# FFN gate/up products: one 512-wide matmul for [high | low] of x, one 256-wide for the low weights

## The chip, the cores and the metric

One core of one Trainium2 chip. The metric is the device time of one execution in microseconds (us), the median of several runs. The inputs and outputs are fp32 arrays in HBM, and the whole program is one launch.

## What is computed

The reference is two stacked blocks on 256 tokens of width 1024. The first is a mixer (neighbourhood attention, Fourier and convolution heads) and a mixture of 32 experts; the second has two layers, each with a feed-forward part (FFN), attention, and another FFN. The change touches the four FFNs only:

```python
def swiglu(x, w_in, w_out):
    gate, up = jnp.split(x @ w_in, 2, axis=-1)      # w_in: 1024 x 5632
    return (jax.nn.silu(gate) * up) @ w_out         # w_out: 2816 x 1024

for i in range(2):
    x = x + 0.5 * swiglu(rmsnorm(x, norm_gains[i, 0]), ffn_w_in[i, 0], ffn_w_out[i, 0])
    ...                                             # dilated, then latent attention
    x = x + 0.5 * swiglu(rmsnorm(x, norm_gains[i, 2]), ffn_w_in[i, 1], ffn_w_out[i, 1])
```

## The kernel before

Large products are done in three passes of a shorter format (fp32r): each fp32 operand is split into a high part, rounded to fp32r, and a low part, the rest; the product is high times high plus high times low plus low times high. For x the parts are XH and XL (128 partitions x 8 k-tiles x 256 tokens each); for the weights they are HI and LO, made from RAW, the buffer that the DMA fills. RAW, HI and LO have two slots, j = 0 and 1.

`ffn` works on chunks of 128 hidden channels. There are 22 of them in an FFN: FF_TWICE = 11 steps i of a loop, two slots j each, so 88 chunks in the four FFNs. A chunk has 128 gate columns and 128 up columns of w_in (2048 elements per partition of the slot, q = 0 for gate and 1 for up) and 128 rows of w_out (1024 elements per partition).

- SyncE (`sync`, L144) issues the loads: as soon as `gu_low` of slot j is done, the next gate/up weights of that slot (L153), and after the low part of the down weights, the next down weights (L156).
- ScalarE (ACT) makes the high parts: `gu_high` (L162, 2048 wide) and the down part (L175, 1024 wide), which waits until the matmuls of the down product of the same slot, one step earlier, no longer need HI. `silu(j, i)` then takes silu of the gate half out of PSUM (L180, into SG), waits for the product with up, and makes its high part HH (L182).
- VectorE (DVE) makes the low parts: `gu_low` (L166) and the down part (L199). `hidden(j, i)` multiplies SG by the up half in PSUM (L205, into H) and makes the low part HL (L207).
- TensorE (PE) runs `gate_up(j, i)`: for q = 0 and 1 and each of the 8 k-tiles three matmuls 256 tokens wide (L232), 48 in all, into one PSUM bank, 4 or 5, gate in one half and up in the other. `down(j, i)` is 12 matmuls 512 wide (L242), which accumulate in banks 0 to 3 over all chunks.

The order on each engine is written out by hand. In a step of the loop:

- PE: gate_up(0, i), down(1, i - 1), gate_up(1, i), down(0, i)
- ACT: gu_high(0, i), down part of high(0, i), silu(1, i - 1), gu_high(1, i), down part of high(1, i), silu(0, i)
- DVE: the low parts and `hidden` in the same order as ACT.

So ACT, after the down product of one slot, makes that slot's down high part, then handles the hidden values of the other slot, and only then makes the gate/up high part for the chunk after next on PE. At the end of an FFN, ACT and DVE handle chunk (1, 10) while PE runs down(0, 10), and down(1, 10) comes last; then DVE adds 0.5 times the result to X (L221). Ahead of each FFN and attention, `norm_and_transpose` squares X on ACT (L94), scales it, transposes it on PE (L123, through banks 6, 7, 2 and 3) and writes XH (ACT, L97) and XL (DVE, L113).

The semaphores named in the change: gu_used (gate_up done), silu (ACT to DVE), h_done (DVE to ACT, and to PE as "the bank is free"), hh_done, hl_done (DVE to PE: HH and HL are ready), dn_used (down done).

Of the kernel before, what the change touches and what calls it, by code (L numbers as in the profile page):

```python
# [16 lines left out]
ALU = mybir.AluOpType  # L17
ACT = mybir.ActivationFunctionType
AX = mybir.AxisListType
f32 = mybir.dt.float32  # L20
f32r = mybir.dt.float32r
i32 = mybir.dt.int32

D = 1024
KT = D // 128
T = 256
# [35 lines left out]
def at_least(eng, sem, value):  # L62

    if not isinstance(value, int) or value > 0:
        eng.wait_ge(sem, value)
# [63 lines left out]
def ffn(nc, M, n_norm, f, w_in, w_out, raw_free):  # L129


    XH, XL, X, PS, s = M.XH, M.XL, M.X, M.PS, M.ffn
    Y = PS[:, 0:4, :]
    GU = [PS[:, 4, :], PS[:, 5, :]]
    w_in_v = w_in.rearrange("(k p) n -> p k n", p=128)
    w_out_v = w_out.rearrange("(c p) n -> c p n", p=128)
    u0 = FF_TWICE * f
    a, v, e, sp = nc.scalar, nc.vector, nc.tensor, nc.sync

    def gu(buf, j):  # L140
        return buf[:, j, 0:2048].rearrange("p (q k n) -> p q k n", q=2, k=KT)

    def dn(buf, j):
        return buf[:, j, 2048:3072]  # L144

    def sync():
        for j in range(2):
            raw_free(sp, j)
        with sp.Fori(0, FF_TWICE) as i:
            for j in range(2):  # L150
                sp.wait_ge(s.gu_lo[j], i + (u0 + 1))
                for q in range(2):
                    sp.dma_start(gu(M.RAW, j)[:, q], w_in_v[:, :, bass.ds(i * 256 + (j * 128 + q * FF), 128)]  # L153
                                 ).then_inc(s.gu_in[j], 16)
                sp.wait_ge(s.dn_lo[j], i + (u0 + 1))
                sp.dma_start(dn(M.RAW, j), w_out_v[bass.ds(i * 2 + j, 1)].rearrange("a p n -> p (a n)")  # L156
                             ).then_inc(s.dn_in[j], 16)

    def gu_high(j, i):
        a.wait_ge(s.gu_in[j], i * 32 + (32 * u0 + 32))  # L160
        a.wait_ge(s.gu_used[j], i + (u0 + 1))
        a.activation(M.HI[:, j, 0:2048], M.RAW[:, j, 0:2048], ACT.Copy).then_inc(s.gu_hi[j], 1)  # L162

    def gu_low(j, i):
        v.wait_ge(s.gu_hi[j], i + (u0 + 1))
        v.tensor_tensor(M.LO[:, j, 0:2048], M.RAW[:, j, 0:2048], M.HI[:, j, 0:2048].bitcast(f32),  # L166
                        ALU.subtract).then_inc(s.gu_lo[j], 1)

    def act():
        def high_parts(j, i, first=False):  # L170
            if not first:
                gu_high(j, i)
            a.wait_ge(s.dn_in[j], i * 16 + (16 * u0 + 16))
            a.wait_ge(s.dn_used[j], i + (u0 + 1))
            a.activation(dn(M.HI, j), dn(M.RAW, j), ACT.Copy).then_inc(s.dn_hi[j], 1)  # L175

        def silu(j, i):
            a.wait_ge(s.gu_used[j], i + (u0 + 2))
            a.wait_ge(s.h_done[j], i + (u0 + 1))
            a.activation(M.SG[:, j], GU[j][:, 0:T], ACT.Silu).then_inc(s.silu[j], 1)  # L180
            a.wait_ge(s.h_done[j], i + (u0 + 2))
            a.activation(M.HH[:, j], M.H[:, j], ACT.Copy).then_inc(s.hh_done[j], 1)  # L182

        high_parts(0, 0, first=True)
        high_parts(1, 0)
        silu(0, 0)
        with a.Fori(1, FF_TWICE) as i:
            high_parts(0, i)
            silu(1, i - 1)
            high_parts(1, i)  # L190
            silu(0, i)
        silu(1, FF_TWICE - 1)

    def dve():
        def low_parts(j, i, first=False):
            if not first:
                gu_low(j, i)
            v.wait_ge(s.dn_hi[j], i + (u0 + 1))
            v.tensor_tensor(dn(M.LO, j), dn(M.RAW, j), dn(M.HI, j).bitcast(f32),  # L199
                            ALU.subtract).then_inc(s.dn_lo[j], 1)  # L200

        def hidden(j, i):
            v.wait_ge(s.silu[j], i + (u0 + 1))
            v.wait_ge(s.dn_used[j], i + (u0 + 1))
            v.tensor_tensor(M.H[:, j], M.SG[:, j], GU[j][:, T:2 * T], ALU.mult).then_inc(s.h_done[j], 1)  # L205
            v.wait_ge(s.hh_done[j], i + (u0 + 1))
            v.tensor_tensor(M.HL[:, j], M.H[:, j], M.HH[:, j].bitcast(f32), ALU.subtract).then_inc(s.hl_done[j], 1)  # L207

        low_parts(0, 0, first=True)
        low_parts(1, 0)  # L210
        hidden(0, 0)
        with v.Fori(1, FF_TWICE) as i:
            low_parts(0, i)
            hidden(1, i - 1)
            low_parts(1, i)
            hidden(0, i)
        hidden(1, FF_TWICE - 1)
        for n in range(4):
            v.wait_ge(s.y_done, 4 * f + n + 1)
            xs = X[:, n // 2, 512 * (n % 2):512 * (n % 2) + 512]  # L220
            v.scalar_tensor_tensor(xs, Y[:, n], 0.5, xs, ALU.mult, ALU.add).then_inc(M.x_ready, 1)  # L221

    def pe():
        def gate_up(j, i, first=False):
            e.wait_ge(s.gu_lo[j], i + (u0 + 2))
            e.wait_ge(s.h_done[j], i + (u0 + 1))
            for q in range(2):
                for k in range(KT):
                    if first and q == 0:
                        e.wait_ge(M.xl_done, KT * n_norm + k + 1)  # L230
                    for n, (w, x) in enumerate([(M.HI, XH), (M.HI, XL), (M.LO, XH)]):
                        m = e.matmul(GU[j][:, T * q:T * q + T], gu(w, j)[:, q, k, :], x[:, k, :],  # L232
                                     start=(k == 0 and n == 0), stop=(k == KT - 1 and n == 2))
            m.then_inc(s.gu_used[j], 1)

        def down(j, i, first=False, last=False):
            e.wait_ge(s.dn_lo[j], i + (u0 + 2))
            e.wait_ge(s.hl_done[j], i + (u0 + 1))
            for t in range(NT):
                for q in range(2):  # L240
                    for n, (h, w) in enumerate([(M.HH, M.HI), (M.HH, M.LO), (M.HL, M.HI)]):
                        m = e.matmul(Y[:, 2 * t + q], h[:, j, 128 * t:128 * t + 128],  # L242
                                     dn(w, j)[:, 512 * q:512 * q + 512],
                                     start=first and n == 0, stop=last and n == 2)
                        if last and (t, q, n) == (1, 1, 1):
                            m.then_inc(s.dn_used[j], 1)
                    if last:
                        m.then_inc(s.y_done, 1)
            if not last:
                m.then_inc(s.dn_used[j], 1)  # L250

        gate_up(0, 0, first=True)
        gate_up(1, 0)
        down(0, 0, first=True)
        with e.Fori(1, FF_TWICE) as i:
            gate_up(0, i)
            down(1, i - 1)
            gate_up(1, i)
            down(0, i)
        down(1, FF_TWICE - 1, last=True)  # L260

    return sync, act, dve, pe, lambda: gu_high(0, 0), lambda: gu_low(0, 0)
# [1802 lines left out]
def program(nc, A, out):  # L2065

    with ExitStack() as c:
        M = Names()

        def sb(name, shape, dtype=f32):  # L2070
            return c.enter_context(nc.sbuf_tensor(name, shape, dtype))
# [12 lines left out]
        M.X = sb("X", [128, NT, D])  # L2084
        M.ID = sb("ID", [128, 128])
        M.GC = sb("GC", [128, N_GC])
        M.XH, M.XL = sb("XH", [128, KT, T], f32r), sb("XL", [128, KT, T], f32r)
        M.RAW = sb("RAW", [128, 2, SLOT])
        M.HI, M.LO = sb("HI", [128, 2, SLOT], f32r), sb("LO", [128, 2, SLOT], f32r)
        M.R = sb("R", [128, 11776])  # L2090
# [17 lines left out]
        def carve(*shape, at=None):  # L2108
            n = math.prod(shape)
            start = end[0] if at is None else at  # L2110
            end[0] = start + n
            assert end[0] <= ARENA
            ap = arena[:, start:start + n]
            if len(shape) == 2:
                return ap.rearrange("p (a b) -> p a b", a=shape[0])
            if len(shape) == 3:
                return ap.rearrange("p (a b c) -> p a b c", a=shape[0], b=shape[1])
            if len(shape) == 4:
                return ap.rearrange("p (a b c d) -> p a b c d", a=shape[0], b=shape[1], c=shape[2])
            return ap  # L2120
# [41 lines left out]
        xn = carve(NT, D, at=0)  # L2162
        ot = carve(KT, T, at=0)
        base = end[0]
        junk, M.SG, M.H = carve(D), carve(2, T), carve(2, T)
        beyond = lambda at, n: M.R[:, KT * D + at:KT * D + at + n]
        M.a_SC = [[carve(384, at=base), carve(768)], [beyond(0, 384), beyond(384, 768)]]
        M.a_PT = [[carve(384), carve(384)], [beyond(1152, 384), beyond(1536, 384)]]
# [234 lines left out]
```

## Time and profile before

| | us |
|---|---|
| median of 3 runs | 2085.25 (2079.49 to 2085.77) |
| the profiled execution | 2084.06 |
| its span, first to last instruction | 2082.2 |

The profiled execution has 1.86 us outside its span. The four FFNs lie at about 768 to 958, 1289 to 1479, 1487 to 1676 and 1888 to 2078 us of the span. In the rows below, "busy" of PE counts pipelined matmuls whose recorded durations overlap, so the pace of PE is read from start to start or from the pieces of the chain, not from the mean duration. PEld is the weight load that goes ahead of each matmul. What stands in brackets at the end of a timeline row is the idle time before the instruction and who ended it.

### The profile page before, as it was taken

How to read it: one execution, taken by the hardware profiler on the slowest of the kernel's cores; microseconds unless marked ns; L12 is line 12 of the kernel's file. 1: busy time of each engine (PE TensorE's matmuls, PEld its weight loads, DVE VectorE, ACT ScalarE, POOL GpSimd, SP SyncE). 2: the span in 40 equal slices, each digit the busy share in tenths (PEclk: the TensorE clock that was granted, in tenths of full speed). 3: DMA queues.
4: the chain of work that ended last, by engine and by line, in shares of the span. 5: the costliest groups of instructions: out<-in, count | busy, mean ns of one | idle time of the engine just before them, and what ended most of it. 6: DMA issues, size and time to landing. Idle time of an engine off the chain costs nothing.

```text
span 2082.2 us, 30499 instructions
## 1 busy us (share of the span) xinstructions
PE 1906.7 (92%) x11508; PEld 1439.0 (69%) x11508; DVE 887.5 (43%) x1391; ACT 734.5 (35%) x1190; POOL 94.9 (5%) x88
## 2 busy tenths in 40 slices
PE   6999699999998959997999998999899977788999
PEld 2875434434333339997999985999899965547998
DVE  4242301111111054545777764454544435525554
ACT  3352212111111134444555543444444434424443
POOL 1000000000000000000111110000000001100000
PEclk8999799999999989999999999999999988879999
DMA  9851699999999956664745442666566550105663
GB/s 366 302 210 63 227 393 393 396 392 395 396 391 396 394 165 183 181 196 121 233 122 152 121 121 60 183 181 181 151 182 183 176 193 0 33 28 152 181 181 111
DMA packets 377285, 441.85 MB, mean 212 GB/s; under 512 B 14469, under 2 KB 273029, under 8 KB 373893
## 3 DMA queue, kind: packets, MB, share of 16 engines
q1 hardware_dynamic: 374776, 431.60, 62.2%
q0 software_dynamic: 2176, 8.39, 1.2%
q10 hardware_dynamic: 272, 1.05, 0.1%
q8 instruction: 38, 0.62, 0.1%
q14 instruction: 23, 0.19, 0.0%
HBM read 439.94 MB, written 1.05 MB: 212 GB/s over the span
## 4 chain that ended last, share of the span: by engine, by line
PE 78%; DMA 10%; ACT 4%; DVE 3%; SPq 2%; issue 2%; POOL 1%; ACTq 0%; POOLq 0%; DVEq 0%
PE PS L232 24%; PE PS L242 11%; PE PS L429 10%; DMA R<-w_up 8%; PE PS L1857 4%; PE PS L1533 4%; PE PS L1835 3%; PE PS L1806 3%; PE PS L1825 3%; SPq L1692 2%; PE PS L757 1%; PE PS L709 1%; PE PS L1642 1%; PE PS L835 1%; ACT ARENA L1723 1%
## 5 line engine op out<-in xcount | busy, mean ns | idle before, releaser
L232 PE MATMUL PS<-XH,HI 128*128 128x256 f32 x1408 | 399.8, 284 | 0.6 <-DVE LO L166 0.6
L232 PE MATMUL PS<-XL,HI 128*128 128x256 f32 x1408 | 398.6, 283 | 0.0
L232 PE MATMUL PS<-XH,LO 128*128 128x256 f32 x1408 | 398.5, 283 | 0.0
L232 PEld LDWEIGHTS PS<-XH,HI 128*128 128x128 f32 x1408 | 270.3, 192 | 4.7 <-DVE LO L166 1.0
L232 PEld LDWEIGHTS PS<-XL,HI 128*128 128x128 f32 x1408 | 270.2, 192 | 3.8
L232 PEld LDWEIGHTS PS<-XH,LO 128*128 128x128 f32 x1408 | 270.2, 192 | 0.0
L166 DVE TENSOR_TENSOR LO<-RAW,HI 128x2048 fp32r<-128x2048 f32 x88 | 201.7, 2292 | 118.8 <-ACT HI L162 118.8
L1777 DVE TENSOR_TENSOR ARENA<-PS,ARENA 128x512 f32<-128x512 f32 x64 | 44.2, 691 | 375.6 <-PE PS L1835 375.6
L175 ACT ACTIVATE HI<-RAW 128x1024 fp32r<-128x1024 f32 x88 | 93.4, 1062 | 295.0 <-PE PS L242 295.0
L199 DVE TENSOR_TENSOR LO<-RAW,HI 128x1024 fp32r<-128x1024 f32 x88 | 107.8, 1225 | 196.8 <-ACT HI L175 196.5
L162 ACT ACTIVATE HI<-RAW 128x2048 fp32r<-128x2048 f32 x88 | 167.8, 1907 | 6.3 <-DMA RAW<-ffn_w_in 6.3
L1825 PE MATMUL PS<-R,ARENA 128*64 128x512 f32 x640 | 144.8, 595 | 13.3 <-DMA R<-w_up 13.3
L242 PE MATMUL PS<-LO,HH 128*128 128x512 f32 x352 | 139.0, 395 | 0.0
L242 PE MATMUL PS<-HI,HL 128*128 128x512 f32 x352 | 139.0, 395 | 0.0
L242 PE MATMUL PS<-HI,HH 128*128 128x512 f32 x352 | 139.0, 395 | 0.0
L429 PE MATMUL PS<-HI,XL 128*128 128x384 f32 x384 | 134.8, 351 | 2.2 <-DVE LO L416 2.2
L429 PE MATMUL PS<-HI,XH 128*128 128x384 f32 x384 | 129.6, 338 | 0.0
L429 PE MATMUL PS<-LO,XH 128*128 128x384 f32 x384 | 129.4, 337 | 0.0
L1825 PEld LDWEIGHTS PS<-R,ARENA 128*64 128x64 f32 x640 | 44.6, 137 | 110.5 <-issue 77.0
L1825 PE MATMUL PS<-RAW,ARENA 128*64 128x512 f32 x384 | 86.7, 594 | 4.0 <-DMA RAW<-w_up 2.4
L1728 ACT ACTIVATE ARENA<-PS 128x512 f32<-128x512 f32 x16 | 9.6, 597 | 225.2 <-PE PS L1825 225.2
L416 DVE TENSOR_TENSOR LO<-RAW,HI 128x3072 fp32r<-128x3072 f32 x24 | 80.5, 3354 | 12.6 <-ACT HI L411 12.6
(310 smaller groups left out, 2946.0 us busy)
## 6 DMA issues: line engine op xcount, KB each, us to landing
RAW<-ffn_w_in SPq DMA_DIRECT2D x176, 512.0 KB, 5.1
RAW<-ffn_w_out SPq DMA_DIRECT2D x88, 512.0 KB, 3.5
R<-w_gate SPq DMA_DIRECT2D x80, 512.0 KB, 11.4
R<-w_up SPq DMA_DIRECT2D x80, 512.0 KB, 10.5
R<-w_down SPq DMA_DIRECT2D x80, 512.0 KB, 12.4
RAW<-a_w_in SPq DMA_DIRECT2D x72, 512.0 KB, 5.3
R<-w_ada SPq DMA_DIRECT2D x24, 1024.0 KB, 7.6
RAW<-w_gate SPq DMA_DIRECT2D x48, 512.0 KB, 13.0
```

The costliest lines, as they stand in the source:

```text
L162: a.activation(M.HI[:, j, 0:2048], M.RAW[:, j, 0:2048], ACT.Copy).then_inc(s.gu_hi[j], 1)
L166: v.tensor_tensor(M.LO[:, j, 0:2048], M.RAW[:, j, 0:2048], M.HI[:, j, 0:2048].bitcast(f32), ALU.subtract).then_inc(s.gu_lo[j], 1)
L175: a.activation(dn(M.HI, j), dn(M.RAW, j), ACT.Copy).then_inc(s.dn_hi[j], 1)
L199: v.tensor_tensor(dn(M.LO, j), dn(M.RAW, j), dn(M.HI, j).bitcast(f32), ALU.subtract).then_inc(s.dn_lo[j], 1)
L232: m = e.matmul(GU[j][:, T * q:T * q + T], gu(w, j)[:, q, k, :], x[:, k, :], start=(k == 0 and n == 0), stop=(k == KT - 1 and n == 2))
L242: m = e.matmul(Y[:, 2 * t + q], h[:, j, 128 * t:128 * t + 128], dn(w, j)[:, 512 * q:512 * q + 512], start=first and n == 0, stop=last and ...
L416: v.tensor_tensor(M.LO[:, slot], M.RAW[:, slot], M.HI[:, slot].bitcast(f32), ALU.subtract).then_inc(s.w_lo[slot], 1)
L429: m = e.matmul(FB[t][:, 0:AW], x[:, k, 128 * t:128 * t + 128], part(w, slot)[:, k].rearrange("p g n -> p (g n)"), start=(k == 0 and n == 0 ...
L1533: mm = e.matmul(FB[n % 2][:, 256 * m:256 * m + 256], l, r, start=(k == 0 and q == 0), stop=(k == KT - 1 and q == 2))
L1806: m = e.matmul(PS[:, 4 + k // 4, 128 * (k % 4):128 * (k % 4) + 128], XN[:, t, 128 * k:128 * k + 128], M.OH[:, t], start=t == 0, stop=t == 1)
L1825: mm = e.matmul((GB, UB)[m // 4][CAP * x:CAP * x + CAP], M.XG[:, k, CAP * x:CAP * x + CAP], w[:, x, kk, :], start=k == 0, stop=k == KT - 1)
L1857: mm = e.matmul(PS[CAP * x:CAP * x + CAP, 2 + q, :], M.HT[:, 128 * f + CAP * x:128 * f + CAP * x + CAP], w[:, x, 512 * q:512 * q + 512], s ...
```

## The change

The 256-wide pair "high weights times high x" and "high weights times low x" becomes one matmul 512 wide, whose moving operand is [XH | XL] of a k-tile, now adjacent in one buffer XHL. Its left half of the bank collects high times high, its right half high times low. The third product, low weights times high x, stays 256 wide and accumulates into the left half. Gate and up so need a bank each, and the two slots take banks 4 and 5, 6 and 7. The halves still have to be added: ACT first copies the two right halves (gate and up, 512 elements per partition) out of PSUM into GH, DVE adds the two left halves from PSUM to them in place, ACT takes silu of the gate part, now in SBUF and in place, and DVE multiplies it by the up part, also in SBUF. HH and HL follow as before. The counts of silu and h_done go up by 2 per chunk instead of 1.

```diff
-    GU = [PS[:, 4, :], PS[:, 5, :]]
+    GU = [PS[:, 4 + 2 * j:6 + 2 * j, :] for j in range(2)]
...
         def silu(j, i):
             a.wait_ge(s.gu_used[j], i + (u0 + 2))
-            a.wait_ge(s.h_done[j], i + (u0 + 1))
-            a.activation(M.SG[:, j], GU[j][:, 0:T], ACT.Silu).then_inc(s.silu[j], 1)
-            a.wait_ge(s.h_done[j], i + (u0 + 2))
+            at_least(a, s.hl_done[j], i + u0)
+            a.activation(M.GH[:, j], GU[j][:, :, T:2 * T], ACT.Copy).then_inc(s.silu[j], 1)
+            a.wait_ge(s.h_done[j], i * 2 + (2 * u0 + 2))
+            a.activation(M.SG[:, j], M.SG[:, j], ACT.Silu).then_inc(s.silu[j], 1)
+            a.wait_ge(s.h_done[j], i * 2 + (2 * u0 + 3))
             a.activation(M.HH[:, j], M.H[:, j], ACT.Copy).then_inc(s.hh_done[j], 1)
...
         def hidden(j, i):
-            v.wait_ge(s.silu[j], i + (u0 + 1))
+            v.wait_ge(s.silu[j], i * 2 + (2 * u0 + 1))
+            v.tensor_tensor(M.GH[:, j], GU[j][:, :, 0:T], M.GH[:, j], ALU.add).then_inc(s.h_done[j], 1)
+            v.wait_ge(s.silu[j], i * 2 + (2 * u0 + 2))
             v.wait_ge(s.dn_used[j], i + (u0 + 1))
-            v.tensor_tensor(M.H[:, j], M.SG[:, j], GU[j][:, T:2 * T], ALU.mult).then_inc(s.h_done[j], 1)
+            v.tensor_tensor(M.H[:, j], M.SG[:, j], M.H[:, j], ALU.mult).then_inc(s.h_done[j], 1)
...
         def gate_up(j, i, first=False):
             e.wait_ge(s.gu_lo[j], i + (u0 + 2))
-            e.wait_ge(s.h_done[j], i + (u0 + 1))
+            at_least(e, s.h_done[j], i * 2 + 2 * u0)
...
-                    for n, (w, x) in enumerate([(M.HI, XH), (M.HI, XL), (M.LO, XH)]):
-                        m = e.matmul(GU[j][:, T * q:T * q + T], gu(w, j)[:, q, k, :], x[:, k, :],
-                                     start=(k == 0 and n == 0), stop=(k == KT - 1 and n == 2))
+                    both = lambda: e.matmul(GU[j][:, q], gu(M.HI, j)[:, q, k, :], M.XHL[:, k].rearrange("p a t -> p (a t)"),
+                                            start=k == 0, stop=k == KT - 1)
+                    rest = lambda: e.matmul(GU[j][:, q, 0:T], gu(M.LO, j)[:, q, k, :], XH[:, k, :], start=False, stop=False)
+                    for product in ((both, rest) if k < KT - 1 else (rest, both)):
+                        m = product()
...
-        M.XH, M.XL = sb("XH", [128, KT, T], f32r), sb("XL", [128, KT, T], f32r)
+        M.XHL = sb("XHL", [128, KT, 2, T], f32r)
+        M.XH, M.XL = M.XHL[:, :, 0], M.XHL[:, :, 1]
...
-        junk, M.SG, M.H = carve(D), carve(2, T), carve(2, T)
+        junk, M.GH = carve(D), carve(2, 2, T)
+        M.SG, M.H = M.GH[:, :, 0], M.GH[:, :, 1]
```

## Rows read from the trace of the kernel before

**Rows 1.** The page: busy times of the engines.

```profile
PE 1906.7 (92%) x11508; PEld 1439.0 (69%) x11508; DVE 887.5 (43%) x1391; ACT 734.5 (35%) x1190; POOL 94.9 (5%) x88
```

**Rows 2.** Stretches: us, then busy (instructions) by engine, PE clock, DMA.

```profile
790.00:940.00 150.00, 150.00 (x1053) 140.31 (x1052) 74.95 (x71) 62.51 (x70) 0.00 (x0) 1.00 0.62 184
```

**Rows 3.** The chain that ended last, in order of time: start, length, what.

```profile
792.01 5.75 PE PS L232 x48
797.76 2.80 PE PS L242 x12
```

**Rows 4.** Timeline of PE, 384-wide fp32r matmuls, the first and last of 21.

```profile
1059.67 0.34 PE L429 MATMUL PS<-HI,XH 128*128 128x384 f32 x1
...
1063.14 0.33 PE L429 MATMUL PS<-LO,XH 128*128 128x384 f32 x1
```

**Rows 5.** Timeline of PE and PEld where two gate_up products begin.

```profile
902.73 0.19 PEld L232 LDWEIGHTS PS<-XH,HI 128*128 128x128 f32 x1
902.96 0.28 PE L232 MATMUL PS<-XH,HI 128*128 128x256 f32 x1
...
911.27 0.19 PEld L232 LDWEIGHTS PS<-XH,HI 128*128 128x128 f32 x1
911.50 0.28 PE L232 MATMUL PS<-XH,HI 128*128 128x256 f32 x1
```

**Rows 6.** Timeline of ACT between those two.

```profile
903.22 1.06 ACT L175 ACTIVATE HI<-RAW 128x1024 fp32r<-128x1024 f32 x1 [3.56 <-PE PS L242]
904.19 0.36 ACT L180 ACTIVATE ARENA<-PS 128x256 f32<-128x256 f32 x1
905.90 0.42 ACT L182 ACTIVATE HH<-ARENA 128x256 fp32r<-128x256 f32 x1 [1.35 <-DVE ARENA L205]
906.23 1.90 ACT L162 ACTIVATE HI<-RAW 128x2048 fp32r<-128x2048 f32 x1
```

**Rows 7.** Timeline of DVE, from the same down part on, and the next chunk's L166.

```profile
904.31 1.22 DVE L199 TENSOR_TENSOR LO<-RAW,HI 128x1024 fp32r<-128x1024 f32 x1 [2.33 <-ACT HI L175]
905.46 0.41 DVE L205 TENSOR_TENSOR ARENA<-ARENA,PS 128x256 f32<-128x256 f32 x1
906.35 0.43 DVE L207 TENSOR_TENSOR HL<-ARENA,HH 128x256 fp32r<-128x256 f32 x1 [0.48 <-ACT HH L182]
908.16 2.29 DVE L166 TENSOR_TENSOR LO<-RAW,HI 128x2048 fp32r<-128x2048 f32 x1 [1.38 <-ACT HI L162]
...
916.79 2.29 DVE L166 TENSOR_TENSOR LO<-RAW,HI 128x2048 fp32r<-128x2048 f32 x1 [1.46 <-ACT HI L162]
```

**Rows 8.** Timeline at the start of the first FFN, where PE does wait for L166.

```profile
772.32 2.29 DVE L166 TENSOR_TENSOR LO<-RAW,HI 128x2048 fp32r<-128x2048 f32 x1 [0.57 <-ACT HI L162]
...
774.66 0.38 PE L232 MATMUL PS<-XH,HI 128*128 128x256 f32 x1 [0.25 <-DVE LO L166]
774.88 0.28 PE L232 MATMUL PS<-XL,HI 128*128 128x256 f32 x1
```

**Rows 9.** Groups by form: the shapes of the added operations on ACT and DVE.

```profile
L1728 ACT ACTIVATE ARENA<-PS 128x512 f32<-128x512 f32 x16 | 9.6, 597 | 225.2 <-PE PS L1825 225.2
L862 ACT ACTIVATE ARENA<-ARENA 128x256 f32<-128x256 f32 x8 | 3.3, 410 | 0.1
L1777 DVE TENSOR_TENSOR ARENA<-PS,ARENA 128x512 f32<-128x512 f32 x64 | 44.2, 691 | 375.6 <-PE PS L1835 375.6
```

**Rows 10.** Timeline of ACT and DVE at the end of the second FFN.

```profile
1472.38 0.38 ACT L180 ACTIVATE ARENA<-PS 128x256 f32<-128x256 f32 x1 [2.59 <-PE PS L232]
...
1473.70 0.43 DVE L207 TENSOR_TENSOR HL<-ARENA,HH 128x256 fp32r<-128x256 f32 x1 [0.48 <-ACT HH L182]
1475.88 2.79 DVE L221 SCALAR_TENSOR_TENSOR X<-PS,X 128x512 f32<-128x512 f32 x4 [1.75 <-PE PS L242]
```

**Rows 11.** Timeline of ACT after the first FFN.

```profile
958.00 2.76 ACT L411 ACTIVATE HI<-RAW 128x3072 fp32r<-128x3072 f32 x1 [5.07 <-DMA RAW<-a_w_in]
```

**Rows 12.** The page's DMA issues: count, KB each, median us to landing.

```profile
RAW<-ffn_w_in SPq DMA_DIRECT2D x176, 512.0 KB, 5.1
```

## The prediction

> **What bounds the kernel now.** I read the page first: PE is busy 92% of the span, DVE 43%, ACT 35% [rows 1]. That only says where to look. The stretch inside the first FFN shows PE busy without a gap at the full clock of 2.4 GHz, DVE half and ACT 42% of the time [rows 2]. The chain of waits there holds nothing but PE: 48 matmuls of gate_up in 5.75 us, 12 of down in 2.80 us, again and again [rows 3]. So 256-wide matmuls go at 5.75 / 48 = 119.8 ns and 512-wide ones at 2.80 / 12 = 233.3 ns from start to start, and a chunk takes 8.55 us. The mean durations in the groups are longer because the matmuls overlap; no saving can be read from them. With PE never waiting, the next question is how near the nearest wait is. That is in the timelines of ACT and DVE between two gate_up starts [rows 5 to 7], and it decides this case.
>
> **What PE gains.** Per k-tile and per gate or up, two 256-wide matmuls (239.6 ns) become one 512-wide (233.3 ns, the pace of L242, which is the same format with the same weight load ahead of each matmul). That is 6.3 ns; times 16 it is 0.10 us per chunk, times 88 chunks 8.9 us. A chunk would take 8.44 us on PE. The gain is small because it is only the fixed part of a matmul: columns stream at 2.4 GHz in 106.7 ns per 256, so the fixed part is 13.1 ns at 256 columns, 173.5 - 160 = 13.5 ns at 384 (3.47 us for 20 intervals [rows 4]), but 20 ns at 512. If the new 512-wide matmul had the fixed part of the 384-wide one it would take 226.8 ns and the gain would be 12.8 ns, 18 us in all. I take 233.3, since it is a row of the very width; the other end goes into a rival.
>
> The Trainium skill (TensorE: Matmul & The Clock Gate, section Back-to-back issue gap) has two figures for this. One is a fixed part of 2.5 ns at any width, by which a pair would save 2.5 ns, 3.5 us in all; the trace has 13 to 20 ns. The other is a sustained 131 ns for a 512-wide matmul among weight loads; the trace has 233.3 ns and so disagrees. By that figure PE would save 108.6 ns a pair, 153 us in all, before ACT and DVE hold it up.
>
> **What ACT and DVE get more of.** Per chunk ACT has a copy of 512 elements from PSUM instead of a silu of 256 from PSUM, and a silu of 256 in SBUF besides: 0.60 and 0.41 us [rows 9] instead of 0.36 [rows 6]. DVE has one add of 512 with a PSUM operand more, 0.69 us, and its multiply reads SBUF only, like L207, 0.43 instead of 0.41 us [rows 9, 7]. In sums that is 57 us on ACT and 62 us on DVE, and by engine load it would be hidden: DVE would be busy some 5.0 of 8.5 us. But it lies in series ahead of the weights' split, so what counts is the path.
>
> **The path.** Take the gate_up that starts at 902.96 [rows 5], call this moment D: the down product before it has ended and freed its high weights. ACT starts the down high part at 903.22 and then silu of the other slot [rows 6]; DVE makes the down low part, ending 905.53, and multiplies, ending 905.87 [rows 7]; ACT makes HH from 905.90 and starts gu_high at 906.23; DVE starts gu_low at 908.16 and ends at 910.45 [rows 6, 7]. These weights are for the gate_up at 911.50, whose first weight load is issued at 911.27 [rows 5]. Handing over from one engine to the other takes 0.03 us; two operations without a wait on one engine overlap by 0.03 to 0.09 us.
>
> After the change: the copy runs 904.19 to 904.79, still under the down low part (hidden; if the low part were shorter by 0.75 us it would show). Then add 905.46 to 906.15, silu 906.18 to 906.59, multiply 906.62 to 907.04, HH from 907.07, gu_high from 907.40, gu_low 909.33 to 911.62. That is 1.17 us later: 0.69 (add) + 0.03 + 0.41 (silu) + 0.03 + 0.01 (multiply). PE, 0.10 us quicker, would want the weights at 911.17; today they are there 0.8 us before the load, then 0.45 us after it. What does PE lose? Where PE waits for L166 today, the low part ends at 774.61, the first matmul starts at 774.66 and the second at 774.88 instead of 0.12 us later [rows 8]: a late start costs 0.05 + 0.10 us behind the end of L166. So the next gate_up counts as started at 911.62 + 0.15 = 911.77, or L = 8.81 us after D, against 8.44 that PE would need by itself. In the other slot D is 911.50 and L166 starts at 916.79 [rows 5, 7]; L166 ends 7.58 us after D instead of 7.49, since the loop's branch is passed on ACT there, so L = 8.90 us.
>
> **How a late path adds up.** The path starts at the end of one down product and ends at the gate_up after the next one. If s is the time between two ends of down products, the next s is 8.44 + max(0, L - s). One late gate_up lengthens s and so gives the next path more room. The first late one in an FFN is gate_up(1, 1), by 0.37 us; after that each pair of chunks loses about 0.37 us together while both are late and 0.46 us once the lateness has settled on one slot. Iterated over the 19 gate_ups that can be late in an FFN, this gives 4.0 us, 16 us in four FFNs. So the loop goes at about 8.44 + 0.20 = 8.64 us per chunk, not 8.55. The first two gate_ups of an FFN are not reached by the path: their ACT and DVE work runs under 5.65 us of gate_up(1, 0) and 2.80 us of down(0, 0).
>
> **The end of an FFN.** The last chunk's hidden values are made under down(0, 10) alone. Today silu starts 1472.38 and HL ends 1474.13 [rows 10]; down(0, 10) starts about 0.2 us before that silu, while the last gate_up matmul drains, and down(1, 10) 2.80 us later, at about 1474.97 with its weight load at 1474.74, so 0.6 us of slack. After: copy 0.60, add 0.69, silu 0.41, multiply 0.43, HH 0.42, HL 0.43 and five handovers of 0.03 to 0.04 make 3.15 us, HL ends at 1475.53, PE is late by 0.05 + 0.10 and effectively starts at 1475.68, 0.7 us late. It passes on to the X updates (L221) and the next stage in three FFNs; after the first one ACT waits for a DMA until 958.00, and X is done at 957.93 and has until 960.7 [rows 11], so there it costs nothing. 3 x 0.7 = 2 us. The hidden values inside the loop are no such place: HL ends at 906.78 now, 907.95 then, and down wants them at 902.73 + 5.65 = 908.38, 0.4 us later.
>
> **What else moves.** The wait of PE for a free PSUM bank is on the add of one chunk of the same slot earlier, long done. Behind ACT's new wait for the add stand silu, HH and gu_high; behind DVE's new wait for silu stand the multiply, HL and gu_low: that is the path above. SyncE's loads follow gu_low and land 5.1 us after their issue [rows 12]; gu_high of the same slot is two chunks on, 17.1 us after gu_high and so 12.9 us after the end of gu_low today, and both of its ends move together, so 1.2 us later costs nothing. XHL changes addresses, not counts, for the attention products. Banks 6 and 7 are read by XH and XL before gate_up(0, 0) can end. Each of these I take as 0, and none has a row that would make it a gain.
>
> **The sum.** 2084.06 - 8.9 + 16 + 2 = 2093.2 us for an execution like the profiled one, which lies 1.2 us under the median of the runs shown; 2094 for the median. Its bounds from rows: a silu of 0.36 (PSUM row) instead of 0.41 and an overlap of 0.03 more give 0.08 x 40 = 3 us less; 0.1 us more of handover per chunk gives 4 us more. Its own range is 2090 to 2099.
>
> **Rivals.**
> - *The 512-wide matmul has the 13.5 ns of the 384-wide row.* For it: two widths agree. Against: the row of the same width. PE gains 18 us and wants 8.34 us a chunk, but the path does not move, so each of the 40 pairs waits 0.10 us more, 20 us instead of 16: 2084 - 18 + 20 + 2 = 2088, or 2089 for the median. No measurable change.
> - *The path is not late.* This decides if the delay of gu_low stays under 0.80 us (8.44 against the 7.49 + 0.15 of today), for which the add and the silu would have to take 0.73 us together instead of 1.10. Then 2084.06 - 8.9 + 2 or less = 2077. Faster. No row is that short, so it gets little.
> - *No gain on PE.* In the new stream a 512-wide and a 256-wide matmul alternate, which the trace does not show. If the weight load behind the 256-wide one is not hidden, or the 512-wide one takes 240 ns, the gain is 0; a chunk wants 8.55 us, stalls are L - 8.55 = 0.26 to 0.35 a pair, 12 us, and the sum is 2084 + 12 + 2 = 2098. Slower.
> - *The path is longer than the sum of its rows.* An in-place operation or the two-bank PSUM operand costs more than a plain one: 0.25 us more on the path adds 0.25 x 40 = 10 us, 2103. Slower.
> - *The new 512-wide matmul goes at the pace of a 256-wide one.* At 119.8 ns PE would want 8.55 - 16 x 0.12 = 6.63 us a chunk, and the path of about 8.85 us would set (8.85 + 6.63) / 2 = 7.74 us, 0.81 us less in each of some 80 chunks, 65 us faster, 2020. Twelve 512-wide matmuls in 2.80 us speak against it. The skill's sustained 131 ns (same page and section) is a figure of this kind; the trace disagrees with it.
>
> **Chances.** Forecast 0.50, 384-like pace 0.17, path not late 0.10, no gain on PE 0.10, longer path 0.12, far faster 0.01. A measurement of this kernel tells about 0.3%, 6.3 us, from no change: slower means over 2091.5. Of the forecast nine tenths lie above that. Slower 0.45 + 0.10 + 0.11 = 0.64 or so, same 0.26, faster 0.10. The range runs from 2081, which takes in the 384-like pace with a shorter path, to 2102.
>
> **What would show it.** In the profile after: L232 in two forms, the 512-wide at 233 ns start to start and the 256-wide at 120; the chain in the FFNs no longer PE alone but passing through L166, gu_high, HH, the multiply, silu and the add; PE waiting for L166 some 55 times by 0.2 to 0.4 us; the add at 0.69, the copy at 0.60, the silu at 0.41 us; the weight load of down(1, 10) waiting for HL. I am wrong if PE's pieces are still gapless, or if the two forms together take less than 345 or more than 360 ns.

## The result and the profile after

| | before | after |
|---|---|---|
| median, us | 2081.4 (2079.49 to 2085.77, 5 runs) | 2094.4 (2093.54 to 2099.85, 5 runs) |
| the profiled execution, its span | 2084.06, 2082.2 | 2099.85, 2098.0 |

The changed kernel is slower: its time is 1.0063 of that of before, interval 1.0044 to 1.0083. With the runs that the experiments below added, the median of before settled at 2084.2 to 2084.6, so by medians the loss is some 10 to 13 us, 0.5 to 0.6%. The forecast was 2094, 0.4 to 0.5% slower. The profiled execution of the changed kernel is the slowest of its five.

The page of the changed kernel, busy times and the groups that answer to [rows 1] and to L232 (columns: busy us, mean ns of one; idle us before and who ended it):

```profile
PE 1911.9 (91%) x10100; PEld 1364.3 (65%) x10100; DVE 949.1 (45%) x1479; ACT 790.9 (38%) x1278; POOL 95.0 (5%) x88
L235 PE MATMUL PS<-XHL,HI 128*128 128x512 f32 x1408 | 503.6, 402 | 11.0 <-DVE LO L166 10.6
L237 PE MATMUL PS<-XHL,LO 128*128 128x256 f32 x1408 | 367.1, 281 | 0.0
```

L235 is the new 512-wide matmul, L237 the 256-wide one. PE now has idle time that L166, the low parts of the gate/up weights, ends; before it was busy without a gap in an FFN [rows 2]. DVE got 62 us of work more and ACT 56, as the rows had it, and both are still under half busy.

The view of the line L235 has the idle time before its matmuls and before its weight loads in one count, so many late starts stand in it twice:

```profile
its engine sat idle before it (us, times) until:
  DVE LO L166: 27.0, 63
  issue: 16.6, 27
```

By the timelines, start to start, 50 of the 80 gate_ups that follow a down product begin late.

The chain that ended last, one gate_up start to the next (start, length, what; answers to [rows 3]). It used to hold PE alone:

```profile
900.13 1.07 ACT HI L175
...
902.37 0.69 DVE ARENA L206
903.06 0.02 issue
903.08 0.43 ACT ARENA L182
903.51 0.02 issue
903.53 0.44 DVE ARENA L209
...
904.38 1.93 ACT HI L162
906.31 0.02 issue
906.34 2.30 DVE LO L166
908.64 0.12 issue
908.76 0.49 PE PS L235
...
914.64 2.81 PE PS L248 x12
```

Once the late starts have settled on one slot, the chain leaves PE every second chunk at the end of a down product and goes down part (L175), add (L206), silu (L182), multiply (L209), high part (L162), low part (L166) before it is back on PE. These are the forecast's links in the forecast's order. The timelines of ACT and DVE in the next chunk answer to [rows 6] and [rows 7]:

```profile
908.54 1.06 ACT L175 ACTIVATE HI<-RAW 128x1024 fp32r<-128x1024 f32 x1 [2.24 <-PE PS L248]
909.51 0.58 ACT L180 ACTIVATE ARENA<-PS 128x512 f32<-128x512 f32 x1
911.50 0.42 ACT L182 ACTIVATE ARENA<-ARENA 128x256 f32<-128x256 f32 x1 [1.41 <-DVE ARENA L206]
...
910.78 0.68 DVE L206 TENSOR_TENSOR ARENA<-PS,ARENA 128x512 f32<-128x512 f32 x1
911.95 0.43 DVE L209 TENSOR_TENSOR ARENA<-ARENA 128x256 f32<-128x256 f32 x1 [0.48 <-ACT ARENA L182]
...
914.67 2.29 DVE L166 TENSOR_TENSOR LO<-RAW,HI 128x2048 fp32r<-128x2048 f32 x1 [1.38 <-ACT HI L162]
```

The copy ends at 910.09, under the down low part, as was said; the add took 0.68 us, the silu 0.42, the multiply 0.43, the handovers 0.02 to 0.04.

And PE where it waits (answers to [rows 5] and [rows 8]):

```profile
908.06 0.39 PE L248 MATMUL PS<-HI,HL 128*128 128x512 f32 x1
...
908.76 0.49 PE L235 MATMUL PS<-XHL,HI 128*128 128x512 f32 x1 [0.32 <-DVE LO L166]
...
909.09 0.28 PE L237 MATMUL PS<-XHL,LO 128*128 128x256 f32 x1
```

Without the wait the gate_up would have started at 908.06 + 0.23 = 908.29. It started 0.47 us later, and its second matmul came 0.33 us behind the first instead of 0.23: 0.57 us lost. (The 0.32 us in brackets is less than 0.47, because it counts from the end of a matmul's recorded duration of 0.39 us, and matmuls in a stream follow each other after 0.23.)

**Where the difference of the two profiled executions lies.** From the start of the first to the start of the last matmul of an FFN, by the timelines:

| FFN | before, us | after, us | change |
|---|---|---|---|
| 1 | 188.44 | 191.63 | +3.2 |
| 2 | 188.73 | 191.65 | +2.9 |
| 3 | 188.84 | 193.49 | +4.7 |
| 4 | 188.50 | 192.23 | +3.7 |

That is 14.5 us. The stages behind the first and the third FFN are 1.8 and 0.7 us shorter than before, and 3.8 us more lie ahead of the first FFN (it starts at 772.2 instead of 768.4). None of these three can be put down to the change: over the ten kernels profiled here the first FFN starts between 767.6 and 773.9 us, with no regard to what was changed in them. The stage behind it, which waits for a DMA [rows 11], took 332.0 us before, but 329.3 in before_reordered and 330.2 in layout_only, whose FFNs are as fast; that DMA took 8.49 us in the profile before, 6.61 in before_reordered and 7.25 in the changed kernel. So the time of the four FFNs, 14.5 us more, is a cleaner measure of the loss than a difference of medians.

### The profile page after: what moved, and what is told of

Its sections match the earlier page's. It is cut to its first block, busy times and chain, and to the rows that moved or that the text cites. A ratio compares the mean times of both kernels' runs of the same rounds, so it can differ in the third digit from the quotient of the medians.

```text
span 2098.0 us, 28187 instructions
## 1 busy us (share of the span) xinstructions
PE 1911.9 (91%) x10100; PEld 1364.3 (65%) x10100; DVE 949.1 (45%) x1479; ACT 790.9 (38%) x1278; POOL 95.0 (5%) x88
## 4 chain that ended last, share of the span: by engine, by line
PE 64%; ACT 9%; DMA 9%; DVE 9%; issue 4%; SPq 2%; POOL 1%; ACTq 0%; DVEq 0%; POOLq 0%
PE PS L235 10%; PE PS L435 9%; DMA R<-w_up 8%; PE PS L248 6%; PE PS L237 5%; PE PS L1863 4%; PE PS L1539 4%; DVE LO L166 4%; ACT HI L162 3%; PE PS L1841 3%; PE PS L1812 3%; PE PS L1831 3%; SPq L1698 2%; ACT HI L175 2%; PE PS L763 1%
## 5 line engine op out<-in xcount | busy, mean ns | idle before, releaser
L235 PE MATMUL PS<-XHL,HI 128*128 128x512 f32 x1408 | 503.6, 402 | 11.0 <-DVE LO L166 10.6
L237 PE MATMUL PS<-XHL,LO 128*128 128x256 f32 x1408 | 367.1, 281 | 0.0
L235 PEld LDWEIGHTS PS<-XHL,HI 128*128 128x128 f32 x1408 | 259.8, 189 | 82.6 <-issue 16.6
L237 PEld LDWEIGHTS PS<-XHL,LO 128*128 128x128 f32 x1408 | 267.0, 190 | 12.7
L166 DVE TENSOR_TENSOR LO<-RAW,HI 128x2048 fp32r<-128x2048 f32 x88 | 201.7, 2292 | 119.8 <-ACT HI L162 119.8
L435 PE MATMUL PS<-HI,XHL 128*128 128x384 f32 x768 | 212.3, 344 | 2.2 <-DVE LO L422 2.2
L175 ACT ACTIVATE HI<-RAW 128x1024 fp32r<-128x1024 f32 x88 | 93.3, 1060 | 205.9 <-PE PS L248 205.9
L162 ACT ACTIVATE HI<-RAW 128x2048 fp32r<-128x2048 f32 x88 | 167.9, 1908 | 5.4 <-DMA RAW<-ffn_w_in 4.8
L1831 PE MATMUL PS<-R,ARENA 128*64 128x512 f32 x640 | 144.8, 595 | 13.2 <-DMA R<-w_up 13.2
L435 PEld LDWEIGHTS PS<-HI,XHL 128*128 128x128 f32 x768 | 141.0, 189 | 8.0 <-issue 4.6
L435 PE MATMUL PS<-LO,XHL 128*128 128x384 f32 x384 | 129.3, 337 | 0.0
L1863 PE MATMUL PS<-R,ARENA 128*64 128x512 f32 x320 | 71.8, 595 | 10.4 <-ACT ARENA L1738 10.4
L182 ACT ACTIVATE ARENA<-ARENA 128x256 f32<-128x256 f32 x88 | 36.8, 418 | 117.6 <-DVE ARENA L206 117.6
```

The lines of the kernel that those rows point to most:

```text
L235: both = lambda: e.matmul(GU[j][:, q], gu(M.HI, j)[:, q, k, :], M.XHL[:, k].rearrange("p a t -> p (a t)"), start=k == 0, stop=k == KT - 1)
L237: rest = lambda: e.matmul(GU[j][:, q, 0:T], gu(M.LO, j)[:, q, k, :], XH[:, k, :], start=False, stop=False)
L435: m = e.matmul(FB[t][:, 0:AW], x[:, k, 128 * t:128 * t + 128], part(w, slot)[:, k].rearrange("p g n -> p (g n)"), start=(k == 0 and n == 0 ...
L1831: mm = e.matmul((GB, UB)[m // 4][CAP * x:CAP * x + CAP], M.XG[:, k, CAP * x:CAP * x + CAP], w[:, x, kk, :], start=k == 0, stop=k == KT - 1)
L1863: mm = e.matmul(PS[CAP * x:CAP * x + CAP, 2 + q, :], M.HT[:, 128 * f + CAP * x:128 * f + CAP * x + CAP], w[:, x, 512 * q:512 * q + 512], s ...
```

## The experiments

The theory is the one of the forecast: PE gains about 0.12 us a chunk, and the longer path from ACT and DVE takes more than that back. The rivals: the new stream of matmuls is no quicker in itself; any operation added to ACT or DVE costs its own time; the new layout of XH and XL costs something elsewhere. "A pair" below is the time from one gate_up to the next of the same slot, two chunks, read from the timelines in the first FFN, where it has settled. "FFNs" is the sum of the four spans from first to last matmul start, as in the table above.

| kernel | median, us | ratio to before (interval) | pair, us | FFNs, us | PE |
|---|---|---|---|---|---|
| before | 2084.2 to 2084.6 | | 17.09 | 754.5 | old stream |
| changed | 2094.4 | 1.0063 (1.0044 to 1.0083) | 17.40 | 769.0 | new |
| pe_only | 2075.29 | 0.9952 (0.9938 to 0.9965) | 16.84 | 743.7 | new |
| path_only | 2102.76 | 1.0086 (1.0072 to 1.0099) | 17.53 | 775.1 | old |
| after_reordered | 2076.66 | 0.9960 (0.9946 to 0.9973) | 16.84 | 746.8 | new |
| before_reordered | 2084.28 | 0.9999 (0.9990 to 1.0008) | 17.09 | 754.1 | old |
| dose1 | 2085.24 | 1.0005 (0.9995 to 1.0015) | 17.09 | 754.3 | old |
| dose3 | 2109.26 | 1.0119 (1.0102 to 1.0136) | 17.74 | 780.3 | old |
| waits_swapped | 2094.51 | 1.0058 (1.0043 to 1.0073) | 17.25 to 17.35, not settled | 768.5 | new |
| layout_only | 2084.86 | 1.0004 (0.9995 to 1.0013) | 17.09 | 754.2 | old |

### PE's part alone

```diff
...
-            a.activation(M.GH[:, j], GU[j][:, :, T:2 * T], ACT.Copy).then_inc(s.silu[j], 1)
-            a.wait_ge(s.h_done[j], i * 2 + (2 * u0 + 2))
-            a.activation(M.SG[:, j], M.SG[:, j], ACT.Silu).then_inc(s.silu[j], 1)
...
+            a.activation(M.SG[:, j], GU[j][:, 0, 0:T], ACT.Silu).then_inc(s.silu[j], 1)
...
-            v.tensor_tensor(M.GH[:, j], GU[j][:, :, 0:T], M.GH[:, j], ALU.add).then_inc(s.h_done[j], 1)
...
-            v.tensor_tensor(M.H[:, j], M.SG[:, j], M.H[:, j], ALU.mult).then_inc(s.h_done[j], 1)
+            v.tensor_tensor(M.H[:, j], M.SG[:, j], GU[j][:, 1, 0:T], ALU.mult).then_inc(s.h_done[j], 1)
...
```

The waits, left out here, count as before the change. The right halves are computed and never read.

> The changed matmuls (512-wide and 256-wide, two banks a slot) with the ACT and DVE work of the kernel before: silu reads the left half of the gate bank, the multiply the left half of the up bank. Left out: the right halves, high weights times low x, are computed by PE but never read. Theory (the path through ACT and DVE costs more than PE gains): with the old path PE never waits, a chunk takes 8.43 us (5.63 for gate_up, 2.80 for down), 88 chunks x 0.12 = 9 to 10 us faster than before, about 0.4 to 0.5%. Rival (the alternating 512- and 256-wide stream is no quicker in itself): 0 to 3 us from before. Rival (512-wide at a much better pace): over 20 us faster.

8.9 us faster by the medians, ratio 0.9952; 10.8 us by the FFNs. Two down products in the chain of waits (start, length, what):

```profile
845.02 2.79 PE PS L244 x12
...
853.44 2.79 PE PS L244 x12
```

They stand 8.42 us apart, against 8.55 before [rows 3]: 5.63 us for gate_up, which is 351.9 ns for a 512-wide and a 256-wide matmul where three 256-wide ones took 359.4. The new stream is quicker in itself, by 7.5 ns where the pace of L242 gave 6.3; the first rival is out.

### The path alone

```diff
-                    both = lambda: e.matmul(GU[j][:, q], ...
-                    rest = lambda: e.matmul(GU[j][:, q, 0:T], ...
...
+                    for n, (w, x, h) in enumerate([(M.HI, XH, 0), (M.HI, XL, T), (M.LO, XH, 0)]):
+                        m = e.matmul(GU[j][:, q, h:h + T], gu(w, j)[:, q, k, :], x[:, k, :],
+                                     start=(k == 0 and n == 0), stop=(k == KT - 1 and n == 2))
```

> The changed ACT and DVE work (copy of the right halves, add, silu in SBUF, multiply), layout and banks, but all three products as 256-wide matmuls as before, high times low x into the right half of the bank. Theory: PE wants 8.55 us a chunk again, the path does not move, so the stalls shrink a little but the gain is gone; a pair of chunks takes about 17.09 + 0.45 us where it has settled, 15 to 20 us slower than before, 5 to 8 us slower than the changed kernel. Rival (the time is lost in the new matmul stream, not in the path): the path alone costs 0 to 3 us.

18.5 us slower than before, 8 us slower than the changed kernel. The chain of waits:

```profile
871.25 1.93 ACT HI L162
873.17 0.02 issue
873.20 2.31 DVE LO L166
875.50 0.12 issue
875.63 6.02 PE PS L236 x48
881.65 2.81 PE PS L246 x12
```

It is the chain of the changed kernel with the old 48 matmuls in it. So the loss is in the path, whatever PE does, and PE's gain is real but half used: the pair is 17.53 us here and 17.40 in the changed kernel, 0.13 us less, where the same matmuls without waits save 0.25.

### The same work in another order

```diff
...
         with a.Fori(1, FF_TWICE) as i:
-            high_parts(0, i)
-            silu(1, i - 1)
-            high_parts(1, i)
-            silu(0, i)
+            gu_high(0, i)
+            silu(1, i - 1)
+            dn_high(0, i)
+            gu_high(1, i)
+            silu(0, i)
+            dn_high(1, i)
...
```

DVE has the same exchange: gu_low, hidden, then the low part of the down weights. Once it was made on the changed kernel, once on the kernel before.

> The changed kernel, and in the loop ACT and DVE handle the hidden values of a slot before the down part of the other slot's weights instead of after it. The wait for the down product then no longer stands ahead of the copy, the add and silu: these start when gate_up ends, 2.8 us earlier. Same operations, same counts. Theory: gu_low ends some 2.5 us before PE wants it, no stall is left in the loop, PE keeps its 9 to 10 us, the end of each FFN still costs 0.7 us in three of four: 7 to 8 us faster than before, 0.35%, and some 19 us faster than the changed kernel. Rival (stalls come from sharing of PSUM or SBUF, not from the order of the work): as slow as the changed kernel, 12 us over before.

> The kernel before with the same reordering of ACT and DVE alone. PE does not wait in its loop, so both theories expect no change: within 2 us of before. If it were faster by 5 us or more, the gain of the reordered changed kernel would not come from the stalls.

On the changed kernel: ratio 0.9960, 2076.66 us, 18 us under the changed kernel and 7.6 us under the kernel before; on the kernel before: no change, to 0.1%. Timelines of ACT and DVE in the reordered changed kernel:

```profile
848.12 0.60 ACT L183 ACTIVATE ARENA<-PS 128x512 f32<-128x512 f32 x1 [2.78 <-PE PS L245]
849.48 0.42 ACT L185 ACTIVATE ARENA<-ARENA 128x256 f32<-128x256 f32 x1 [0.76 <-DVE ARENA L214]
850.39 0.42 ACT L187 ACTIVATE HH<-ARENA 128x256 fp32r<-128x256 f32 x1 [0.49 <-DVE ARENA L217]
850.89 1.06 ACT L178 ACTIVATE HI<-RAW 128x1024 fp32r<-128x1024 f32 x1
851.86 1.90 ACT L162 ACTIVATE HI<-RAW 128x2048 fp32r<-128x2048 f32 x1
...
853.79 2.29 DVE L166 TENSOR_TENSOR LO<-RAW,HI 128x2048 fp32r<-128x2048 f32 x1 [0.58 <-ACT HI L162]
```

and the chain of waits there:

```profile
856.43 2.79 PE PS L258 x12
```

The copy (L183) now follows the end of gate_up at once, where ACT used to sit waiting for the down product. gu_low (L166) ends at 856.08, and its gate_up starts 2.79 us after the down product at 856.43, at 859.2: 3.1 us of room. All added operations are still there, with the same durations to 0.02 us, so what cost the time in the loop was only where they stood. This kernel beats the one before and the changed one. Its FFNs take 3.1 us more than those of pe_only, which is the late last down product, 0.77 us in each of the four, that the order in the loop does not touch (1.4 us by the medians).

### The slack by itself

```diff
             v.tensor_tensor(M.H[:, j], M.SG[:, j], GU[j][:, T:2 * T], ALU.mult).then_inc(s.h_done[j], 1)
+            for m in range(3):                            # 1 in dose1
+                v.wait_ge(s.h_done[j], i * 4 + (4 * u0 + m + 2))
+                v.tensor_tensor(M.H[:, j], M.H[:, j], M.H[:, j], ALU.max).then_inc(s.h_done[j], 1)
...
```

The counts of h_done that the other engines wait for go up with it.

> The kernel before, with one operation of DVE more on the path and nothing else: after the multiply, an in-place maximum of H with itself (256 elements in SBUF, about 0.43 us and 0.04 of waiting), which leaves the values as they are. It measures the slack of the path by itself. Theory: the slack in the loop is 0.7 to 0.8 us and at the end of an FFN 0.6 us, so 0.47 us more is covered: no change, within 2 us. Rival (any operation on the path costs its own time, or part of it): 88 x 0.47 = 41 us, or half of it.

> The kernel before with three such operations in a row on the path, 1.4 us in all, 0.25 us more than the change adds, and PE's stream as it was. Theory: 0.6 us over the slack; a late start of PE costs about 0.15 to 0.23 us more; a pair of chunks loses 0.6 to 0.7 us once, not twice; 40 pairs and three ends of 0.9 us: 22 to 28 us slower than before. If each chunk lost the whole excess it would be 50 to 55 us; if the time is lost elsewhere in the change, 0 to 3 us.

One operation costs nothing that can be measured, ratio 1.0005; three cost 24.6 us. The three in DVE's timeline:

```profile
896.74 0.42 DVE L205 TENSOR_TENSOR ARENA<-ARENA,PS 128x256 f32<-128x256 f32 x1
897.19 1.34 DVE L208 TENSOR_TENSOR ARENA<-ARENA 128x256 f32<-128x256 f32 x3
```

They put 1.36 us on the path. With the slack of 0.8 us and the late start the pair should grow by 0.6 to 0.7 us; it grew by 17.74 - 17.09 = 0.65. So the cost of the path is not proportional to the work on it: nothing up to the slack, then once per pair of chunks. Neither busy time (113 us more on DVE by the pages, 1000.1 against 887.5) nor a loss in every chunk fits.

### The two waits exchanged, and the layout

```diff
-            e.wait_ge(s.gu_lo[j], i + (u0 + 2))
             at_least(e, s.h_done[j], i * 2 + 2 * u0)
+            e.wait_ge(s.gu_lo[j], i + (u0 + 2))
```

> The changed kernel with the two waits at the head of gate_up exchanged: first for the free bank, always long met, then for the low weights. In the changed kernel's trace, in one of the two slots, register arithmetic for the bank's wait stands behind the wait for the low weights, and the first matmul starts 0.13 us after the low part ends instead of 0.05. Theory: each of the 40 pairs gets back up to 0.08 us, 0 to 3 us faster than the changed kernel, hardly to be told by the time, but the first matmul of a late gate_up then starts 0.05 us after the low part in both slots. Rival (the 0.13 us is the restart of a 512-wide matmul): it stays 0.13.

2094.51 us and 768.5 us in the FFNs, no gain that can be told, and the expectation on the mechanism failed: one slot still starts late. DVE's L166, and the load that waited for it:

```profile
875.23 2.29 DVE L166 TENSOR_TENSOR LO<-RAW,HI 128x2048 fp32r<-128x2048 f32 x1 [1.38 <-ACT HI L162]
...
877.64 0.19 PEld L235 LDWEIGHTS PS<-XHL,HI 128*128 128x128 f32 x1 [0.39 <-issue]
```

877.52 to 877.64, 0.12 us to the load, where the other slot took 0.05. But it is not the same slot as before the exchange. In the changed kernel all late gate_ups of slot 0 start 0.13 us after L166 ends and those of slot 1 0.05; here those of slot 0 start after 0.05, those of slot 1 after 0.15. The trace shows why: the load carries only one of its two waits, and the other is an instruction of PE's queue ahead of it. In slot 0 the load carries the later of the two in the program, in slot 1 the earlier. So the exchange put slot 0 right and spoiled slot 1. Why the two slots differ in this was not tried.

```diff
-        M.XH, M.XL = sb("XH", [128, KT, T], f32r), sb("XL", [128, KT, T], f32r)
+        M.XHL = sb("XHL", [128, KT, 2, T], f32r)
+        M.XH, M.XL = M.XHL[:, :, 0], M.XHL[:, :, 1]
```

> The kernel before with XH and XL adjacent per k-tile in one buffer, nothing else. The part ahead of the first FFN took 3.8 us longer in the profiled run of the changed kernel and the attention products read the new layout. Theory: a single run's scatter, and the layout costs nothing: within 2 us of before. Rival (the layout costs something in the products outside of the FFNs): 3 to 4 us slower.

Ratio 1.0004, interval up to 1.0013: the layout costs nothing that can be told. Dose1 has the old layout and its first FFN starts at 773.3 us, later than in the changed kernel: the 3.8 us ahead of it were that execution's.

## Why the prediction was right

- **PE's gain.** Forecast 0.10 us a chunk; measured (17.09 - 16.84) / 2 = 0.125 us in pe_only. That is 11 us in 88 chunks, and 10.8 by the FFNs, against a forecast of 8.9; that the medians of pe_only and before differ by just 8.9 is luck. The 512-wide row was the right one to take, not the 384-wide one: with 226.8 ns a pair of chunks would have saved 0.41 us, and it saved 0.25.
- **Load of ACT and DVE.** 56 and 62 us more, hidden in after_reordered but for the ends of the FFNs. The forecast's separation of load and path is what the reordering shows.
- **The path.** L166 was forecast to end 8.66 and 8.75 us after the end of the down product (8.81 and 8.90 less the 0.15 of the late start). In the first FFN the down products end at 908.29 and 8.42 us earlier, at 899.87; L166 ends at 916.96 and 908.63, so 8.67 and 8.76 us. The sum of link by link was exact there, because each added operation had a row of its own shape and the handovers had been read from the same chain. In the other FFNs one slot takes longer, 8.75 and 8.75 us in the second, 8.86 and 8.75 in the third (9.12 in its first chunk), 8.76 and 8.84 in the fourth. The operations last as long as in the first FFN. The added time is in the handover from the silu to the multiply of one slot, 0.12 us in the second and fourth FFN and 0.21 in the third instead of 0.03, and in the fourth the high part (L162) of the other slot starts 0.08 us later. The chain of the third FFN:

```profile
1600.78 0.43 ACT ARENA L182
1601.20 0.03 issue
1601.23 0.04 DVEq L208
1601.27 0.14 issue
1601.41 0.44 DVE ARENA L209
```

  An instruction of DVE's queue stands between them, as at the slow start of PE. No row from before could show it: there the silu has long ended when DVE comes to the multiply [rows 6, 7]. Why it differs from one FFN to the next was not tried.
- **The stalls.** This term of the sum was too small: forecast 16 us. In the trace 50 gate_ups start late, 17.5 us in all, and their second matmuls add 5.0: 22.5 us. ((17.40 - 16.84) x 40 = 22 says the same.) The largest part of the difference is the late start: 0.15 us in the forecast, taken from the one place where PE waited for L166 [rows 8], outside the loop. In the loop it is 0.15 us in one slot and 0.13 + 0.10 = 0.23 in the other (the fence with 908.76 above), and except in the third FFN it is this other slot that settles as the late one: 8.76 + 0.23 + 8.42 = 17.41 us a pair in the first, against 17.34 in the forecast. An estimate, by iterating the forecast's own rule with the measured sizes: 17.3 us with PE's 8.42 us a chunk, 20.2 with the late start of 0.23 as well, 22.1 with the path of each FFN as it was.
- **The end of an FFN.** Forecast 0.7 us each. The changed kernel shows the wait that was named, here at the end of the second FFN:

```profile
1482.08 0.39 PE L248 MATMUL PS<-HI,HL 128*128 128x512 f32 x1
1482.44 0.43 DVE L211 TENSOR_TENSOR HL<-ARENA,HH 128x256 fp32r<-128x256 f32 x1 [0.48 <-ACT HH L184]
1483.01 0.47 PE L248 MATMUL PS<-HI,HH 128*128 128x512 f32 x1 [0.54 <-DVE HL L211]
1483.32 0.39 PE L248 MATMUL PS<-LO,HH 128*128 128x512 f32 x1
```

  The down product would have started at 1482.08 + 0.23 = 1482.31; it started 0.70 us later, and its second matmul another 0.07 late. It is the same in all four FFNs, 3.1 us in their sum. Behind the first it costs the next stage nothing, as was said: X is done at 964.94, and ACT is kept by the data of the DMA until 965.80.
- **The sum.** For the FFNs alone: -10.8 (PE) + 22.5 (stalls) + 3.1 (ends) = 14.8, and 14.5 measured, against -8.9 + 16 + 2 = 9.1. The gain and the stalls were both put too low, and the two errors cancel in part. That the median came out within 1 us of 2094 is luck as well: it is a median of five in a spread of 6 us. The mechanism, the sign and the path were right.
- **Two slips in the working.** The chances of "slower", 0.45 + 0.10 + 0.11, add up to 0.66, not 0.64, and the iteration with 8.44, 8.81 and 8.90 gives 4.1 us an FFN, not 4.0. Of the signs named, the waits came 50 times against some 55, and by some 0.5 us where settled and not 0.2 to 0.4.

The rivals that lost: path not late (dose1 and dose3 put the slack between 0.45 and 1.36 us, and the add and silu exceed it), no gain on PE (pe_only), a faster stream (pe_only), a path longer than its rows by 0.25 us (8.67 and 8.76 in the first FFN, and once settled up to 0.2 us more than that in one slot of the others, which is a handover and no operation).

## What to carry to other kernels

An engine that is never idle in the profile can be near a wait: before adding work to engines that are half idle, read how long before its use the last of their products is ready (0.8 us here), and add the new operations link by link on that path. If they do not fit, look first for the wait that stands ahead of them in the queue without need: moved behind it, the same operations cost nothing in the loop, and 10 us of loss became 8 us of gain. Read the handovers in every call of the loop: a second wait ahead of an operation made one of them 0.2 us in the third FFN and 0.03 in the first. A late path that returns every second chunk is paid once per pair, because a stall gives the next path more room.

## What was not expected of the hardware

- A matmul whose weight load waits starts 0.05 us after the instruction that frees it where the load carries the wait, and 0.13 to 0.15 us after it where the wait stands as an instruction ahead of the load; the second matmul follows 0.10 us late in the first two cases and 0.07 where the first took 0.15. Exchanging the two waits in the program moved the slow start from slot 0 to slot 1.
- The same shows on DVE: the multiply started 0.03 us after the silu in the first FFN, and 0.21 in one slot of the third, with an instruction of the queue between.
- A 512-wide and a 256-wide fp32r matmul in alternation take 351.9 ns together, about 1 ns less than their paces apart (233.3 and 119.8).
